# Two rows of token scales sent through DRAM on GpSimd's queue instead of through TensorE, in a two-block transformer kernel

## The chip, the cores and the metric

One NeuronCore of a Trainium2 chip runs the whole kernel. The metric is the time of one execution on the device in microseconds (us). The kernel before takes 914.07 us, the median of 3 runs (914.02 to 915.09).

## What is computed

The input is 256 tokens of width 1024 (float32), beside two memories of 256 tokens. Two blocks run one after the other: each is a mixer, a cross-attention on a memory and a feed-forward, every one behind an RMS norm and added to the running state. The two places that matter here are the input projections of the second block's mixer and of its feed-forward, which is the last layer of the kernel:

```python
x = x + hybrid_mixer(rms_norm(x, norm_mix_g), w_in, ...)      # q, k, v, z, ... = split(h @ w_in)
x = x + memory_cross_attention_2(rms_norm(x, norm_xa_g), ...)
x = x + swiglu(rms_norm(x, norm_ffn_g), w_gate, w_up, w_down) # (silu(h @ w_gate) * (h @ w_up)) @ w_down
return rms_norm(x, final_g)
```

`rms_norm` multiplies each token by one number, 1 / sqrt(mean(x^2) + eps). The kernel doesn't apply it ahead of a projection. It multiplies the raw state by the gain, projects, and puts the token's scale on the result, so that the scale can be worked out while TensorE is at the projection.

## The kernel before, in words

**Weights.** All matrices come as 146 slabs of 1 MB through a ring of four buffers (`w_ring`, `load`, L405, on SyncE's queue). ScalarE rounds a slab to `w_hi` (`hi`, L1227), VectorE takes the rest into `w_lo` (`lo`, L1719), and TensorE makes each product in three passes from the two halves of both operands. A slab is loaded into the place of slab i - 4 when TensorE has used that one (`slab_used`).

**Layouts.** A projection comes out either with tokens on the partitions, where a token's scale is a number per partition (`r_mix2`, `r_ff2`: 128 partitions x 2 blocks of tokens), or with features on the partitions and tokens along the free axis (`form_a`, L609 to L611, and `form_a_pair`, L646 and L650). There the scales are needed as a row of 256 numbers repeated on all 128 partitions: `r_row[:, 0, :]`.

**How the row is made.** `scales_on_diagonal(r)` on VectorE (L1756) writes for each block of tokens a 128 x 128 matrix with the scales on the diagonal. `spread` on TensorE (L744 to L751) multiplies a matrix of ones with it, so that every partition of a PSUM bank holds the row. `row_copy` on ScalarE (L1260 to L1262) copies it to `r_row`. It is done for four rows: ROW_MIX and ROW_CONV (first block, which the change leaves alone), ROW_MIX2 (second mixer) and ROW_FF2 (last feed-forward).

**Order around ROW_MIX2** (slabs I_SBQK to I_SBQK + 3 are q and k, I_SBV the two slabs of v). Every engine's order is written out by hand. TensorE: I_SBQK, + 1, + 2, then `spread`, then I_SBQK + 3, for which it waits until VectorE has summed the halves of I_SBQK + 1 (`sum_halves`, L2122), then the two slabs of I_SBV, then I_ZU. VectorE: `r_mix2` (last step L2115), the diagonal, `lo(I_SBQK + 3)`, `sum_halves(1)`, `lo(I_SBQK + 4)`, `sum_halves(2)`, the wait for the row (L2137), `scaled_qk(0)` to `(2)` (L2131), and then `lo(I_SBQK + 5)`, which TensorE needs for the second slab of I_SBV. ScalarE: `row_copy` stands between `half_of(I_SBQK + 2)` and `hi(I_SBQK + 6)`.

**Order around ROW_FF2.** TensorE: gate and up of the first group of 256 hidden columns (I_FF2, I_FF2 + 1), `spread`, gate and up of the second group (`glu_in(ff2_gate(1))`), then `glu_out`, the down-projection of the first group (slab I_FF2 + 4, L609 to L611), for which it waits for `glu_lo` and for that slab's `w_lo`. VectorE: `r_ff2`, then inside `boundary` one more slab (`lo(nxt + 3)`), the diagonal, two `half_add` (L2328), the wait for the row (L2340), and `glu(0)`: gate times row (L2341), gate times up (L2353), `ff_l` (L2358), `lo(nxt + 2)`, which is slab I_FF2 + 4. ScalarE in `glu(0)`: Silu (L1659), `ff_h` (L1668), `hi(nxt + 2)`.

**GpSimd** has done its constants and the rotary angles by then. Its queue holds a few DMAs that repeat a row of DRAM on all partitions: two final gains (L521, `load_gain`), `ln_g`, `ln_b`, `b_sp` (L590 to L592), and at the start one that brings the 256 positions to 128 x 2, one number at a time (L535, `pos_i`). Its last instruction is the load of the last gain, which waits for VectorE's `gain_used` (L2107).

Of the kernel before, what the change touches and what calls it, by code (L numbers as in the profile page):

```python
# [28 lines left out]
F32 = mybir.dt.float32  # L29
# [6 lines left out]
P = 128  # L36
D = 1024
S = 256
# [65 lines left out]
ROW_MIX, ROW_CONV, ROW_MIX2, ROW_FF2 = range(4)  # L104
# [65 lines left out]
def build(nc, a, out):  # L170

    with ExitStack() as ctx:
# [7 lines left out]
        def new(name, shape, dt=F32):  # L180
            t = at(name, shape, cursor[0], dt)
            cursor[0] += -(-int(np.prod(shape[1:])) // 8) * 8
            return t
# [22 lines left out]
        r_row = new("r_row", [P, 2, S])  # L206
# [88 lines left out]
        def stats(n):  # L295
            used[0] += n
            assert used[0] <= 256
            return stat[:, used[0] - n:used[0]]
# [5 lines left out]
        r_mix, r_mem, r_mem2, r_xa, r_mlp, r_f, r_mix2, r_ff2 = (stats(2) for _ in range(8))  # L304
# [6 lines left out]
        def tok(b):  # L311
            return ps[:, b, :]
# [25 lines left out]
        def sem(name):  # L338
            return ctx.enter_context(nc.semaphore(name))
# [13 lines left out]
        diag_ready, row_t, row_ready = sem("diag_ready"), sem("row_t"), sem("row_ready")  # L353
# [33 lines left out]
        gate_ready, merge_done, merged_hi, merged_lo = sem("gate_ready"), sem("merge_done"), sem("merged_hi"), sem("merged_lo")  # L387
        last_sq, sum_ready, root_ready, y_ready, out_lead, out_tail, stored = (sem(x) for x in ("last_sq", "sum_ready", "root_ready", "y_ready", "out_lead", "out_tail", "stored"))
        u_scaled = sem("u_scaled")
        gain_product, last_gain = sem("gain_product"), sem("last_gain")  # L390

        block = ctx.enter_context(nc.Block())
# [122 lines left out]
        def _(pool):  # L515
            def load_gain(n):
                if n > 0:
                    pool.wait_ge(gain_used, n)
                w = a[GAIN_ROWS[n]]
                w = w if len(w.shape) == 1 else w.squeeze(0)  # L520
                pool.dma_start(gain[:, :], w.partition_broadcast(P)).then_inc(gain_loaded, 16)  # L521
# [49 lines left out]
            for part in (TWO_PI_A, TWO_PI_B, TWO_PI_C):  # L571
# [17 lines left out]
            load_gain(G_F)  # L589
            pool.dma_start(ln_g[:, :], a["sgu_ln_g_2"].squeeze(0).partition_broadcast(P)).then_inc(sgu_loaded, 16)  # L590
            pool.dma_start(ln_b[:, :], a["sgu_ln_b_2"].squeeze(0).partition_broadcast(P)).then_inc(sgu_loaded, 16)
            pool.dma_start(b_sp[:, :, :], a["b_spatial_2"].squeeze(0).rearrange("g t -> (g t)").partition_broadcast(P)  # L592
                           .rearrange("p (g t) -> p g t", g=SGU_GROUPS)).then_inc(sgu_loaded, 16)

# [4 lines left out]
            pool.wait_ge(xo_ready, XA_HEADS)  # L599
            pool.memset(y3_pad[:, :, 0:CONV3 - 1], 0.0).then_inc(pad3_ready, 1)  # L600
            load_gain(G_FINAL)


        @block.tensor
        def _(pe):
# [32 lines left out]
            def form_a_pair(i, bank, step=0, ready=(), low_ready=None):  # L638

                pe.wait_ge(hi_done, weight_count(i) + step)  # L640
                wh, wl = slab(i, 256)
                for k in range(KD):
                    if ready:
                        ready(k)
                    for b in range(2):
                        pe.matmul(feat(bank + b), wh[:, k, b * P:(b + 1) * P], xx[:, k, :, :].rearrange("p e t -> p (e t)"), start=k == 0, stop=False)  # L646
                pe.wait_ge(lo_done, weight_count(i) + step)
                for b in range(2):
                    for k in range(KD):
                        mm = pe.matmul(feat(bank + b)[:, 0:S], wl[:, k, b * P:(b + 1) * P], xx[:, k, 0, :], start=False, stop=k == KD - 1)  # L650
                mm.then_inc(slab_used, 1)
# [88 lines left out]
            def raw_ready(n):  # L740

                return [lambda k, done=done: pe.wait_ge(done, 16 * (n - R_XA) + 9 + k) for done in (raw_hi, raw_lo)]

            def spread(m, bank):  # L744

                pe.wait_ge(ones_set, 1)
                pe.wait_ge(const_ready, 1)
                for tb in range(TB):
                    pe.wait_ge(diag_ready, 2 * m + tb + 1)
                    mm = pe.matmul(bank[:, tb * P:(tb + 1) * P], ones[:, :], diag[:, tb, :], start=True, stop=True)  # L750
                mm.then_inc(row_t, 1)  # L751
# [287 lines left out]
            form_a(I_SBQK, (0,), x_t, 256, 0, *raw_ready(R_MIX2))  # L1039
            form_a_pair(I_SBQK + 1, 2)  # L1040
            form_a_pair(I_SBQK + 2, -4)
            spread(ROW_MIX2, tok(3))
            pe.wait_ge(pair_sum, FF_PAIRS + 1)
            form_a_pair(I_SBQK + 3, 2)
            pe.wait_ge(pair_sum, FF_PAIRS + 2)
# [53 lines left out]
            form_a_pair(I_ZU, 0)  # L1099
            pe.wait_ge(pair_sum, FF_PAIRS + 3)  # L1100
            form_a_pair(I_ZU + 1, 2)
            pe.wait_ge(row_ready, 2)
            form_b_half(I_ZV, 2, x_t)
            beside(I_ZV + 1)
            for j in range(4):
# [26 lines left out]
            for n, br in enumerate(BRANCH_ORDER):  # L1132
                for half in range(2):
                    i = I_BR + 6 * n + 3 * half
                    r = 2 * n + half
# [15 lines left out]
                    for kk in range(4):  # L1151
                        for tb in range(TB):
                            t = slice(tb * P, (tb + 1) * P)
# [19 lines left out]
            def glu_in(i, gate_done=None, up_done=None, step=0, ready=(), last=False):  # L1173
                if gate_done is not None:
                    pe.wait_ge(glu_sum, 2 * gate_done - 1)
                form_a_pair(i, 0, step, *ready[1:])
                if up_done is not None:
                    pe.wait_ge(glu_sum, 2 * up_done)
                if last:
                    form_a(i + 1, (2,), x_t, step=step)  # L1180
                else:
                    form_a_pair(i + 1, 2, step)
# [4 lines left out]

            pe.wait_ge(xo_lo, 8)
            glu_in(I_FF2, ready=raw_ready(R_FF2))
            spread(ROW_FF2, tok(0))  # L1190
            glu_in(ff2_gate(1), gate_done=1, up_done=1)
            pe.wait_ge(row_ready, 3)
            glu_out(ff2_gate(1) + 2, 1, first=True)
            with pe.Fori(0, 2) as t:
                for c in range(2, 6):
# [18 lines left out]
        def _(act):  # L1214
# [45 lines left out]
            def row_copy(m, bank):  # L1260
                act.wait_ge(row_t, m + 1)
                act.activation(r_row[:, 0, :], bank[:, 0:S], ACT.Copy).then_inc(row_ready, 1)  # L1262
# [145 lines left out]
            for tb in range(TB):  # L1408
                t = slice(tb * P, (tb + 1) * P)
# [152 lines left out]
            half_of(I_SBQK + 1, 6, qk_half[1])  # L1562
            hi(I_SBQK + 5)
            half_of(I_SBQK + 2, 0, qk_half[2])
            row_copy(ROW_MIX2, tok(3))
            hi(I_SBQK + 6)
            half_of(I_SBQK + 3, 6, qk_half[3])
            hi(I_SBQK + 7)
# [35 lines left out]
            for n in range(BRANCHES):  # L1604
                for half in range(2):
                    i = I_BR + 6 * n + 3 * half
                    r = 2 * n + half
# [36 lines left out]

            half_copy(0, I_FF2)
            half_copy(1, I_FF2 + 1)
            row_copy(ROW_FF2, tok(0))

            def glu(g, i, first=False, last=False, step=0, turn=0):

# [55 lines left out]
        def _(dve):  # L1706
# [47 lines left out]
            def scales_on_diagonal(r):  # L1754
                for tb in range(TB):
                    dve.tensor_scalar(diag[:, tb, :], ident[:, :], r[:, tb:tb + 1], None, ALU.mult).then_inc(diag_ready, 1)  # L1756
# [130 lines left out]
            t = [rope_t[:, j, :, :].rearrange("p t (g f) -> p t g f", f=ROPE_HALF) for j in range(4)]  # L1887
# [95 lines left out]
            for tb in range(TB):  # L1983
                t = slice(tb * P, (tb + 1) * P)
# [9 lines left out]
            for tb in range(TB):  # L1994
                t = slice(tb * P, (tb + 1) * P)
                dve.tensor_tensor(c_acc[:, :, t], c_acc[:, :, t], feat(2)[:, t].unsqueeze(1).broadcast_to([P, 4, P]), ALU.mult).then_inc(conv_normed, 1)
            lo(29)
            for tb in range(TB):
                t = slice(tb * P, (tb + 1) * P)
# [113 lines left out]
            after(dve.tensor_scalar(nv, nv, 1.0 / D, EPS, ALU.mult, ALU.add))  # L2113
            rsqrt(nv, r_mix2, nt)
            after(dve.tensor_tensor(r_mix2, r_mix2, r_f, ALU.mult))  # L2115
            scales_on_diagonal(r_mix2)
            lo(I_SBQK + 3)

            def sum_halves(n, bank, dst):
# [14 lines left out]
            sum_halves(1, 6, qkT2[:, 2:4, :])  # L2134
            lo(I_SBQK + 4)
            sum_halves(2, 0, qkT2[:, 4:6, :])
            dve.wait_ge(row_ready, 2)  # L2137
            for j in range(3):
                scaled_qk(j)
            lo(I_SBQK + 5)  # L2140
# [59 lines left out]
            for tb in range(TB):  # L2200
                dve.wait_ge(vg_ready, tb + 1)
                six, two = bn6[:, 6 * tb:6 * tb + 6], bn2[:, 2 * tb:2 * tb + 2]
                v, y, t = nv[:, tb:tb + 1], ny[:, tb:tb + 1], nt[:, tb:tb + 1]
# [81 lines left out]
            for n in range(BRANCHES):  # L2285
                for half in range(2):
                    i = I_BR + 6 * n + 3 * half
                    r = 2 * n + half
# [14 lines left out]
                    m = merged[:, :, half * HALF:(half + 1) * HALF]  # L2303
# [16 lines left out]
            after(dve.tensor_scalar(r_xa, r_xa, XA_SCALE, None, ALU.mult))  # L2320
            x_attention(1, I_O2)
            boundary(R_FF2, UPD[I_O2], I_O2 + 3, Q_FF2, r_ff2, I_FF2)
            scales_on_diagonal(r_ff2)

            def half_add(c, n):

# [7 lines left out]
            def glu(g, i, first=False, last=False, step=0):  # L2334

                nxt = ff2_gate(1) if first else i + 3
                if not first:
                    half_add(0, 2 * g + 1)
                if first:
                    dve.wait_ge(row_ready, 3)  # L2340
                dve.tensor_tensor(blocks(ff_u[:, 1, :]), blocks(ff_s[:, 0, :]), row_of_scales(0), ALU.mult).then_inc(glu_in_ready, 1)  # L2341
                if last:
                    lo(N_SLABS - 1)
                elif not first:
                    lo(nxt, step)
                if last:
                    dve.wait_ge(slab_used, i + 2 + step)
                elif not first:
                    half_add(1, 2 * g + 2)
                dve.wait_ge(silu_ready, g + 1)  # L2350
                if not first:
                    dve.wait_ge(glu_lo, g)
                dve.tensor_tensor(ff_u[:, 0, :], feat(2) if last else ff_s[:, 1, :], ff_r[:, 0, :], ALU.mult).then_inc(glu_ready, 1)  # L2353
                if not first and not last:
                    lo(nxt + 1, step)
                dve.wait_ge(glu_hi, g + 1)
                f = slice(2, 4) if last else slice(0, 2)
                dve.tensor_tensor(ff_l[:, f, :], blocks(ff_u[:, 0, :]), ff_h[:, f, :].bitcast(F32), ALU.subtract).then_inc(glu_lo, 1)  # L2358
                if not last:
                    lo(nxt + 2, step)  # L2360
# [85 lines left out]
```

## Time and profile before

| | |
|---|---|
| median of 3 runs | 914.07 us |
| span of the profiled execution, first to last instruction | 910.9 us |
| the profiled execution's own time | not recorded; 3.2 us lie between its span and the median |
| TensorE busy with matmuls | 901.4 us, 99% of the span |
| VectorE, ScalarE, GpSimd busy | 661.6, 504.2, 24.3 us |
| DMA | 164.38 MB, mean 180 GB/s |
| granted TensorE clock | 0.999 of full speed |

Lines of the profile give a start and a duration on one engine. PE is TensorE's matmuls, PEld its weight loads, DVE VectorE, ACT ScalarE, POOL GpSimd, SPq SyncE's DMA queue. L with a number is the line of the kernel; helpers such as `lo` give one line for all their uses. Matmuls are pipelined, so one that starts every 0.23 us is shown 0.39 us long.

### The profile page before, as it was taken

How to read it: one execution, taken by the hardware profiler on the slowest of the kernel's cores; microseconds unless marked ns; L12 is line 12 of the kernel's file. 1: busy time of each engine (PE TensorE's matmuls, PEld its weight loads, DVE VectorE, ACT ScalarE, POOL GpSimd, SP SyncE). 2: the span in 40 equal slices, each digit the busy share in tenths (PEclk: the TensorE clock that was granted, in tenths of full speed). 3: DMA queues.
4: the chain of work that ended last, by engine and by line, in shares of the span. 5: the costliest groups of instructions: out<-in, count | busy, mean ns of one | idle time of the engine just before them, and what ended most of it. 6: DMA issues, size and time to landing. Idle time of an engine off the chain costs nothing.

```text
span 910.9 us, 12836 instructions
## 1 busy us (share of the span) xinstructions
PE 901.4 (99%) x5160; PEld 787.4 (86%) x5160; DVE 661.6 (73%) x920; ACT 504.2 (55%) x584; POOL 24.3 (3%) x69
## 2 busy tenths in 40 slices
PE   9999999999999999999999999999999999999997
PEld 8888998889888888888888988888899888888886
DVE  5799999987577666656967996646686676565665
ACT  6796435655555444445656757744464654544444
POOL 1600010000000000000000000000000000000000
PEclk9999999999999999999999999999999999999999
DMA  9746555454355666654755455455453456666551
GB/s 353 253 159 223 183 199 185 139 185 140 92 186 186 195 199 197 190 185 153 238 188 183 159 166 183 152 175 187 173 185 103 144 183 191 196 193 197 189 185 47
DMA packets 101280, 164.38 MB, mean 180 GB/s; under 512 B 2736, under 2 KB 71088, under 8 KB 101104
## 3 DMA queue, kind: packets, MB, share of 16 engines
q1 hardware_dynamic: 100528, 161.71, 54.2%
q0 software_dynamic: 560, 1.84, 0.7%
q8 instruction: 34, 0.56, 0.3%
q10 hardware_dynamic: 144, 0.16, 0.1%
q14 instruction: 14, 0.11, 0.0%
HBM read 162.65 MB, written 1.05 MB: 180 GB/s over the span
## 4 chain that ended last, share of the span: by engine, by line
PE 92%; DVE 5%; DMA 2%; ACT 1%; issue 1%; SPq 0%; DVEq 0%; ACTq 0%
PE ps L609 20%; PE ps L611 19%; PE ps L610 19%; PE ps L646 18%; PE ps L650 9%; DVE w_lo L1719 1%; DVE c_acc L1865 1%; DMA w_ring<-in_w_in 1%; PE ps L737 1%; DMA head_raw<-in_head 1%; PE ps L857 0%; ACT w_hi L1227 0%; PE ps L774 0%; DVE mem_l L1734 0%; PE ps L826 0%
## 5 line engine op out<-in xcount | busy, mean ns | idle before, releaser
L1719 DVE TENSOR_TENSOR w_lo<-w_ring,w_hi 128x2048 fp32r<-128x2048 f32 x146 | 333.4, 2288 | 114.2 <-ACT w_hi L1227 113.2
L1227 ACT ACTIVATE w_hi<-w_ring 128x2048 fp32r<-128x2048 f32 x146 | 278.6, 1911 | 88.3 <-DMA w_ring<-in_w_in 27.3
L646 PE MATMUL ps<-xx,w_hi 128*128 128x512 f32 x720 | 171.8, 391 | 0.3
L646 PEld LDWEIGHTS ps<-xx,w_hi 128*128 128x128 f32 x720 | 133.3, 188 | 27.4 <-issue 0.7
L609 PE MATMUL ps<-w_hi,xx 128*128 128x512 f32 x304 | 120.2, 395 | 0.0
L611 PE MATMUL ps<-w_hi,xx 128*128 128x512 f32 x304 | 118.6, 390 | 0.0
L610 PE MATMUL ps<-w_lo,xx 128*128 128x512 f32 x304 | 118.5, 390 | 0.0
L650 PEld LDWEIGHTS ps<-xx,w_lo 128*128 128x128 f32 x720 | 92.3, 191 | 3.5
L650 PE MATMUL ps<-xx,w_lo 128*128 128x256 f32 x720 | 93.4, 283 | 0.0
L609 PE MATMUL ps<-w_hi,ff_h 128*128 128x512 f32 (+1 forms) x218 | 84.7, 389 | 0.0
L610 PE MATMUL ps<-w_lo,ff_h 128*128 128x512 f32 (+1 forms) x218 | 84.6, 388 | 0.0
L611 PE MATMUL ps<-w_hi,ff_l 128*128 128x512 f32 (+1 forms) x218 | 84.4, 387 | 0.0
L611 PEld LDWEIGHTS ps<-w_hi,xx 128*128 128x128 f32 x304 | 57.1, 188 | 12.1
L609 PEld LDWEIGHTS ps<-w_hi,xx 128*128 128x128 f32 x304 | 57.1, 188 | 11.7 <-issue 0.5
L610 PEld LDWEIGHTS ps<-w_lo,xx 128*128 128x128 f32 x304 | 57.2, 188 | 11.1
L609 PE MATMUL ps<-xx,w_hi 128*128 128x256 f32 x200 | 56.9, 285 | 0.0
L610 PE MATMUL ps<-xx,w_hi 128*128 128x256 f32 x200 | 56.6, 283 | 0.0
L611 PE MATMUL ps<-xx,w_lo 128*128 128x256 f32 x200 | 56.6, 283 | 0.0
L1865 DVE SCALAR_TENSOR_TENSOR c_acc<-u_pad,cols,c_acc 128x256 f32<-128x256 f32 x120 | 49.3, 476 | 0.2 <-DVE stat L1727 0.2
L611 PEld LDWEIGHTS ps<-w_hi,ff_l 128*128 128x128 f32 x218 | 40.9, 188 | 8.5
L609 PEld LDWEIGHTS ps<-w_hi,ff_h 128*128 128x128 f32 x218 | 41.0, 188 | 8.1 <-DVE ff_l L2080 0.2
L610 PEld LDWEIGHTS ps<-w_lo,ff_h 128*128 128x128 f32 x218 | 41.0, 188 | 7.6
(339 smaller groups left out, 1335.9 us busy)
## 6 DMA issues: line engine op xcount, KB each, us to landing
w_ring<-in_w_in SPq DMA_DIRECT2D x34, 1024.0 KB, 5.1
w_ring<-in_mlp_up_w SPq DMA_DIRECT2D x16, 1024.0 KB, 5.6
w_ring<-in_mlp_down_w SPq DMA_DIRECT2D x16, 1024.0 KB, 4.9
w_ring<-in_w_gate_ffn SPq DMA_DIRECT2D x11, 1024.0 KB, 5.3
w_ring<-in_w_up_ffn SPq DMA_DIRECT2D x11, 1024.0 KB, 5.3
w_ring<-in_w_down_ffn SPq DMA_DIRECT2D x11, 1024.0 KB, 4.9
w_ring<-in_xkv_w SPq DMA_DIRECT2D x8, 1024.0 KB, 5.4
w_ring<-in_w_out SPq DMA_DIRECT2D x8, 1024.0 KB, 4.8
```

What stands on the lines that cost most here:

```text
L609: pe.matmul(o, lh, rh, start=first, stop=False)
L610: pe.matmul(o, lh, rl, start=False, stop=False)
L611: return pe.matmul(o, ll, rh, start=False, stop=last)
L646: pe.matmul(feat(bank + b), wh[:, k, b * P:(b + 1) * P], xx[:, k, :, :].rearrange("p e t -> p (e t)"), start=k == 0, stop=False)
L650: mm = pe.matmul(feat(bank + b)[:, 0:S], wl[:, k, b * P:(b + 1) * P], xx[:, k, 0, :], start=False, stop=k == KD - 1)
L737: mm = pe.transpose(ps[:, bank, (k - k0) * P:(k - k0 + 1) * P], h[:, tb, k * P:(k + 1) * P], ident[:, :])
L1227: act.activation(w_hi[:, s, :], w_ring[:, s, :], ACT.Copy).then_inc(hi_done, 1)
L1719: dve.tensor_tensor(w_lo[:, s, :], w_ring[:, s, :], w_hi[:, s, :].bitcast(F32), ALU.subtract).then_inc(lo_done, 1)
L1865: ins = dve.scalar_tensor_tensor(c_acc[:, c, :], win, tap, c_acc[:, c, :], ALU.mult, ALU.add)
```

## The change

For ROW_MIX2 and ROW_FF2 the diagonals, `spread` and `row_copy` are taken out. VectorE raises a semaphore where the diagonals stood. GpSimd, at the end of its program, waits for it, writes the 256 scales to a row of a DRAM tensor, waits until that has landed, and reads the row back into `r_row[:, 0, :]` on all 128 partitions. VectorE waits for that second DMA where it waited for `row_copy`.

```diff
+        scales_ready, row_moved = sem("scales_ready"), sem("row_moved")
...
+            def scales_row(m, r):
+
+                row = a["scales"][m - ROW_MIX2]
+                pool.wait_ge(scales_ready, m - 1)
+                pool.dma_start(row.rearrange("(t p) -> p t", p=P), r, allow_slow_non_contiguous=True).then_inc(row_moved, 16)
+                pool.wait_ge(row_moved, 32 * (m - ROW_MIX2) + 16)
+                pool.dma_start(r_row[:, 0, :], row.partition_broadcast(P)).then_inc(row_moved, 16)
...
             load_gain(G_FINAL)
+            scales_row(ROW_MIX2, r_mix2)
+            scales_row(ROW_FF2, r_ff2)
...
             form_a_pair(I_SBQK + 2, -4)
-            spread(ROW_MIX2, tok(3))
...
             form_a_pair(I_ZU + 1, 2)
-            pe.wait_ge(row_ready, 2)
...
             glu_in(I_FF2, ready=raw_ready(R_FF2))
-            spread(ROW_FF2, tok(0))
             glu_in(ff2_gate(1), gate_done=1, up_done=1)
-            pe.wait_ge(row_ready, 3)
...
             half_of(I_SBQK + 2, 0, qk_half[2])
-            row_copy(ROW_MIX2, tok(3))
...
             half_copy(1, I_FF2 + 1)
-            row_copy(ROW_FF2, tok(0))
...
             after(dve.tensor_tensor(r_mix2, r_mix2, r_f, ALU.mult))
-            scales_on_diagonal(r_mix2)
+            dve.sem_inc(scales_ready, 1)
...
-            dve.wait_ge(row_ready, 2)
+            dve.wait_ge(row_moved, 32)
...
             boundary(R_FF2, UPD[I_O2], I_O2 + 3, Q_FF2, r_ff2, I_FF2)
-            scales_on_diagonal(r_ff2)
+            dve.sem_inc(scales_ready, 1)
...
-                    dve.wait_ge(row_ready, 3)
+                    dve.wait_ge(row_moved, 64)
...
+    aps["scales"] = nc.dram_tensor("scales", (2, S), F32, kind="Internal").ap()
```

## Rows read from the trace of the kernel before

**Rows 1.** The page: the span, and TensorE's busy time with its share of it

```profile
span 910.9 us, 12836 instructions
PE 901.4 (99%) x5160; PEld 787.4 (86%) x5160; DVE 661.6 (73%) x920; ACT 504.2 (55%) x584; POOL 24.3 (3%) x69
```

**Rows 2.** Who waited for whom, TensorE's matmuls: us in total, times, longest

```profile
PE ps L821 <- POOL ones L524: 1.1, 1, 1.1
...
PE ps L609 <- DVE w_lo L1719: 0.5, 1, 0.5
```

**Rows 3.** Chain that ended last, at the two spreads: start us, us, what

```profile
451.25 0.45 PE ps L750 x4
...
732.84 0.44 PE ps L750 x4
```

**Rows 4.** By tile, diagonals and row copies: ns min/median/max, first and last start

```profile
L1756 DVE TENSOR_SCALAR diag<-ident,stat x8: 278/282/290, 24.8 to 732.0; 128x128 f32<-128x128 f32 x8
...
L1262 ACT ACTIVATE r_row<-ps x3: 377/379/386, 30.1 to 733.4; 128x256 f32<-128x256 f32 x3
```

**Rows 5.** Timeline at the second mixer: start us, us, engine, line, operation [idle before]

```profile
447.59 0.16 DVE L2115 TENSOR_TENSOR stat<-stat 128x2 f32<-128x2 f32 x1
...
450.39 0.68 DVE L2122 TENSOR_TENSOR qkT<-ps,qkT 128x512 f32<-128x512 f32 x1
...
454.07 0.68 DVE L2131 SCALAR_TENSOR_TENSOR qkT<-ps,r_row 128x512 f32<-128x512 f32 x1
...
455.87 2.29 DVE L1719 TENSOR_TENSOR w_lo<-w_ring,w_hi 128x2048 fp32r<-128x2048 f32 x1
...
462.57 0.39 PE L609 MATMUL ps<-w_hi,xx 128*128 128x512 f32 x1
```

**Rows 6.** Timeline at the last feed-forward, same columns

```profile
729.60 2.29 DVE L1719 TENSOR_TENSOR w_lo<-w_ring,w_hi 128x2048 fp32r<-128x2048 f32 x1
...
732.56 0.53 PEld L750 LDWEIGHTS ps<-diag,ones 128*128 128x128 f32 x4
...
734.30 0.69 DVE L2341 TENSOR_TENSOR ff_u<-ff_s,r_row 128x512 f32<-128x512 f32 x1
...
736.99 1.90 ACT L1227 ACTIVATE w_hi<-w_ring 128x2048 fp32r<-128x2048 f32 x1
...
738.92 2.29 DVE L1719 TENSOR_TENSOR w_lo<-w_ring,w_hi 128x2048 fp32r<-128x2048 f32 x1 [1.11 <-ACT w_hi L1227]
...
744.15 0.19 PEld L609 LDWEIGHTS ps<-w_hi,ff_h 128*128 128x128 f32 x1
```

**Rows 7.** DMA issues: queue, times, KB each, us from issue to landing

```profile
gain<-in_norm_f_w POOLq DMA_DIRECT2D x1, 512.0 KB, 4.1
gain<-in_final_g POOLq DMA_DIRECT2D x1, 512.0 KB, 5.7
...
out<-xn ACTq DMA_DIRECT2D x1, 160.0 KB, 2.3
pos_i<-in_positions POOLq DMA_DIRECT2D x1, 1.0 KB, 5.4
```

**Rows 8.** Timeline: VectorE ends its work, GpSimd issues the last gain

```profile
438.15 2.36 DVE L2105 TENSOR_TENSOR xn<-h,gain 128x1024 f32<-128x1024 f32 x2
...
440.86 0.53 POOL L521 DMA_DIRECT2D gain<-in_final_g  x1 [198.47 <-DVEq L2107]
```

**Rows 9.** DMA queues from 440 to 444.3 us: packets, MB, share of 16 engines

```profile
q1 hardware_dynamic: 461, 0.94, 70.7%
```

**Rows 10.** Stretches of the last feed-forward: us, busy by engine, PEclk, DMA share, GB/s

```profile
732.00:734.00 2.00, 2.00 (x15) 1.87 (x15) 1.30 (x4) 1.11 (x3) 0.00 (x0) 1.00 0.00 0
734.00:737.70 3.70, 3.70 (x21) 3.17 (x21) 2.23 (x4) 2.93 (x4) 0.00 (x0) 1.00 0.93 279
737.70:739.40 1.70, 1.70 (x14) 1.57 (x13) 0.59 (x2) 1.69 (x2) 0.00 (x0) 1.00 0.03 10
739.40:743.40 4.00, 4.00 (x23) 3.48 (x22) 3.10 (x3) 0.92 (x3) 0.00 (x0) 1.00 0.87 262
```

## The prediction

> **What bounds the kernel now.** I read the page first: TensorE is busy in 901.4 of 910.9 us [rows 1]. The list of waits says that what is left isn't waiting on others: the longest wait of a matmul is 1.1 us at the start, and the only other wait I show is 0.5 us for a `w_lo` [rows 2]. So the kernel is one unbroken queue of matmuls. Work taken from TensorE shortens it by its own length, work taken from VectorE or ScalarE by nothing, and a wait that reaches TensorE lengthens it in full. The reader is to keep two questions apart: what the spreads cost TensorE, and whether a row that comes later reaches TensorE as a wait. The chain of waits answers the first, the timelines and the DMA views the second.
>
> **Removed from TensorE.** The chain that ended last passes through both spreads, for 0.45 and 0.44 us [rows 3]. TensorE must be free to use them. At the mixer it goes on only when the sum at L2122 is ready, which ends at 451.07 [rows 5], just after the spread begins; the two diagonals ahead of it on VectorE, 2 x 0.28 us one behind the other, about 0.4 us on the timeline since their ends overlap [rows 4], go too, so the sum comes at about 450.7. At the feed-forward the sum that TensorE needs moves by the same 0.4 us. I take 0.45 at each place: **-0.9 us** if no row is late. The diagonals and the row copies (0.38 us each on ScalarE, [rows 4]) are worth nothing by themselves; TensorE's 99% covers them. The waits for `row_ready` on TensorE had long been met and cost nothing.
>
> **Added.** Each row now takes: VectorE's semaphore to GpSimd, a scattered store of 1 KB, a semaphore, a read of 128 KB onto 128 partitions, a semaphore. VectorE to GpSimd took 0.35 us for the last gain (440.51 to 440.86, [rows 8]). The two other hops I estimate at 0.1 us. That last gain stands ahead in GpSimd's program; it landed 5.7 us after 440.86 [rows 7], at 446.6, before the first scales are ready, and nothing stands behind the new DMAs. GpSimd's waiting therefore delays only the rows.
>
> The store and the read are not in the trace. From above the nearest rows are `pos_i`, the same 256 single numbers the other way, at 5.4 us, and a gain at 5.7; from below the shortest DMA of all, 2.3 us [rows 7]. The first gain, 512 KB in 4.1 us, bears on both: a slab of 1 MB moves in some 3.7 us (279 GB/s, [rows 10]), half a slab in 1.9, so some 2.2 us are fixed. That gives 2.2 + 0.5 = 2.7 for 128 KB and, with `pos_i`'s issue being slower, about 2.5 for the store, where the DMA engines are free. They often aren't. The last gain was issued at 440.86, yet until 444.3 the DMA engines moved packets of queue 1, the slab loads, alone [rows 9]. I read this as a rule of this kernel: a DMA of GpSimd waits for the slab that is under way. Here the Trainium skill says otherwise ("DMA: Bandwidth & Descriptors", Queues, rings and completion order): each DMA engine takes turns between its queues after every packet, by which the small DMAs would hardly wait; that is a rival below.
>
> **The mixer's row.** The scales are there at 447.75, GpSimd issues at 448.1. With the middles between free and caught (2.5 to 5.4: 4.0; 2.7 to 5.7: 4.2) and two hops the row lands at 456.5, where it was wanted at 454.07 [rows 5]. Behind VectorE's wait stand three scalings and `lo(I_SBQK + 5)`: before, 454.07 to 458.16, so 4.1 us. It would now end at 460.7. TensorE wants that slab at 462.57 [rows 5], now 462.1. Cover: 1.4 us. With both ends high (5.4 + 5.7) the row lands at 459.4 and TensorE waits 1.5 us. I take no wait: **-0.45 us**.
>
> **The feed-forward's row.** VectorE's semaphore comes behind `lo(nxt + 3)`, which ends at 731.89 [rows 6], 2.3 us after the scales are known. GpSimd issues at 732.24. The DMA engines are idle from 732 to 734 [rows 10]; the store's packets pass ahead of the next slab, and it lands at 734.75. The read is issued at 734.85, in the middle of that slab, which holds the engines until 737.7 [rows 10]; 0.5 us of its own data and some 0.2 to land: 738.4, and VectorE goes on at 738.5, not at 734.30. From there the chain can be read off: L2341 starts at 734.30, Silu, the product and `ff_h` follow, ScalarE's `w_hi` runs 736.99 to 738.89, VectorE's `w_lo` of the slab for `glu_out` ends at 741.21 [rows 6]. That is 6.9 us from the row to a ready slab; before, it ended 2.9 us ahead of TensorE's need at 744.15. Now it ends at 745.4, so `glu_out` starts about 745.45, 1.3 us later than before: the saved 0.45 is gone too, and TensorE stands for 1.75 us. **+1.3 us**. With 2.3 for both DMAs it starts at 744.0 (-0.15), with 5.4 and 5.7 at 750.5 (+6.35). Later groups don't add to this: behind `glu_out` come 5.5 us of matmuls, before the next sum is wanted, and VectorE is idle for a third of these stretches [rows 10].
>
> **Sum**: -0.45 + 1.3 = +0.85 us. The span of the profiled execution, 910.9, becomes 911.8; the median stands 3.2 us above that span, and with the same distance it becomes 914.9. With all bounds low -0.6, with all high +7.85.
>
> **Rivals.**
>
> 1. *The row is hardly late.* The read takes turns with the slab: 734.85 + 2.7 = 737.55, chain to 744.55, +0.45 at the feed-forward, 0.0 in sum: 914.1. With both DMAs at 2.3: 913.5. The overtaking is against rows 9. By the skill's rule of turns and the same page's (Anatomy of one DMA) 2.0 us fixed plus bytes at 436 GB/s, an estimate from the page alone gives a row at 736.8 and 913.2.
>
> 2. *Slower: the store is caught as well.* Place: GpSimd's queue at 734. It decides from the point where the store's packets are ready later than 734.0, that is over 1.75 us after the issue. Then the store follows the slab and lands at 738.2, the read is issued at 738.3 and lands at 741.0 if it is ahead of the next slab: chain to 748.0, +3.9, sum +3.4, 917.5. If the read is caught as well (the next slab moves from about 739.4 to 743.4, [rows 10]) it lands at 744.2, `glu_out` starts at 751.3, +7.1, sum +6.7, 920.8. `pos_i`, caught in the loads of the start, with 5.4 us, speaks for it; the idle stretch 732 to 734 against it. TensorE would then stand for 4.3 to 7.5 us; the granted clock is 1.00 in all stretches here [rows 10], and whether it falls after such a gap the trace doesn't show.
>
> 3. *The mixer's row is late too*: up to +1.5 us there in place of 0, so +2.8 in sum, 916.9. Both DMAs must take over 9.7 us together.
>
> 4. *The change does nothing where it says*: TensorE can't use the freed 0.45 us because another wait (the sum at L2122, or a slab) ends last there. Then +0.9 on the sum, 915.8.
>
> **Chances.** The likeliest case 0.45 (its own range 913.9 to 915.8), rival 1 0.17, rival 2 0.29, rival 3 0.05, rival 4 0.04. About 0.2% of the time, 1.8 us, is what a measurement of this kernel can tell from no change. The likeliest case with rivals 1 and 4 stays within it but for the late end of the first: 0.57. Slower by more: rivals 2 and 3 and that end, 0.40. Faster by more than 1.8 us needs twice what both spreads cost: 0.03. Predicted is the likeliest case, 914.9. The range goes from 913.3, both rows in time, to 920.8, both DMAs of the feed-forward caught.
>
> **What the profile after would show.** L750 gone in both places and TensorE going on 0.45 us earlier behind I_SBQK + 2. Two issues of about 0.9 and 0.5 us on POOL at 448 and 732, each pair over 5 to 8 us apart from issue to last landing. L2131 starting at about 456 without a gap on TensorE at 462. L2341 near 738, VectorE idle for some 4 us ahead of it, and a gap of 1.5 to 2 us ahead of L609 where it stood at 744.15, put down to VectorE's `w_lo`. I am wrong if that gap is absent (rows in time) or longer than 3 us, if the row's landing doesn't follow the end of a slab, or if there is a gap at the mixer.

## The result and the profile after

The changed kernel takes 931.39 us (median of 4 runs, 930.16 to 931.57) against 914.05 for before: a ratio of 1.019, 95% interval 1.0178 to 1.0202. I had forecast 914.9 with a range to 920.8. The mechanism of the forecast is there (the row is late, and TensorE stands ahead of `glu_out`), but at both places and several times as long.

The page of the changed kernel, to be read against [rows 1]:

```profile
span 929.8 us, 12817 instructions
...
PE 905.3 (97%) x5152; PEld 789.9 (85%) x5152; DVE 660.9 (71%) x916; ACT 503.3 (54%) x582; POOL 27.1 (3%) x73
...
PEclk9999999999999999999989999999999979999999
```

The span grew by 18.9 us, the median by 17.3. The difference lies in the kernel before: the execution of it that was profiled was a quick one. In the later rounds its executions with a span of 910.9 us took 912.9 to 913.1 us, 2.0 to 2.2 above the span, and not the 3.2 that I had added. TensorE's busy time grew too, although work was taken from it; the clock row says why: in two slices the granted clock is below 0.9. Who waited for whom, in us in total, times and longest:

```profile
POOL r_row L599 <- DMA scales<-stat: 17.1, 2, 9.0
PE ps L620 <- DVE w_lo L1724: 15.3, 3, 8.5
DVE ff_u L2346 <- DMA r_row<-scales: 11.2, 1, 11.2
...
DVE qkT L2136 <- DMA r_row<-scales: 10.1, 1, 10.1
```

Together they are the path of the loss: GpSimd waits for its store, VectorE for the read, and TensorE for a `w_lo` that stands behind VectorE's wait. In [rows 2] the same matmul line (L609 there, L620 here) waited 0.5 us. The DMA issues, KB each and median us from issue to landing:

```profile
r_row<-scales POOLq DMA_DIRECT2D x2, 128.0 KB, 6.5
...
scales<-stat POOLq DMA_DIRECT2D x2, 1.0 KB, 9.0
```

The timeline at the mixer, beside [rows 5]:

```profile
448.42 0.74 POOL L597 DMA_DIRECT2D scales<-stat  x1 [6.71 <-DVEq L2121]
...
458.13 0.57 POOL L599 DMA_DIRECT2D r_row<-scales  x1 [8.97 <-DMA scales<-stat]
...
462.67 1.91 ACT L1234 ACTIVATE w_hi<-w_ring 128x2048 fp32r<-128x2048 f32 x1 [8.85 <-DMA w_ring<-in_w_in]
...
464.62 0.69 DVE L2136 SCALAR_TENSOR_TENSOR qkT<-ps,r_row 128x512 f32<-128x512 f32 x1 [10.08 <-DMA r_row<-scales]
...
466.43 2.29 DVE L1724 TENSOR_TENSOR w_lo<-w_ring,w_hi 128x2048 fp32r<-128x2048 f32 x1
...
468.77 0.79 PE L620 MATMUL ps<-w_hi,xx 128*128 128x512 f32 x1 [6.13 <-DVE w_lo L1724]
```

The scaling starts at 464.62 and not at 454.07; the second slab of v starts at 468.77 and not at 462.57. A line that I had not looked for is ScalarE's: it waited 8.85 us for a slab, so the slab loads are late as well. The timeline at the last feed-forward, beside [rows 6]:

```profile
737.62 2.29 DVE L1724 TENSOR_TENSOR w_lo<-w_ring,w_hi 128x2048 fp32r<-128x2048 f32 x1
737.95 0.72 POOL L597 DMA_DIRECT2D scales<-stat  x1 [279.26 <-DVEq L2328]
...
746.80 0.56 POOL L599 DMA_DIRECT2D r_row<-scales  x1 [8.13 <-DMA scales<-stat]
...
753.50 0.69 DVE L2346 TENSOR_TENSOR ff_u<-ff_s,r_row 128x512 f32<-128x512 f32 x1 [11.24 <-DMA r_row<-scales]
...
758.08 2.29 DVE L1724 TENSOR_TENSOR w_lo<-w_ring,w_hi 128x2048 fp32r<-128x2048 f32 x1 [1.11 <-ACT w_hi L1234]
...
760.52 0.76 PE L620 MATMUL ps<-w_hi,ff_h 128*128 128x512 f32 x1 [8.53 <-DVE w_lo L1724]
```

And the stretches of TensorE's two gaps with what follows each (us, busy by engine, PEclk, DMA share, GB/s):

```profile
462.60:468.70 6.10, 0.04 (x1) 0.00 (x0) 4.08 (x5) 4.30 (x3) 0.00 (x0) 0.75 0.89 308
468.70:472.60 3.90, 3.83 (x9) 3.05 (x10) 3.87 (x5) 0.00 (x0) 0.00 (x0) 0.52 0.00 0
751.90:760.40 8.50, 0.09 (x1) 0.00 (x0) 4.40 (x5) 3.54 (x4) 0.00 (x0) 0.73 0.58 203
760.40:766.00 5.60, 5.48 (x13) 4.35 (x14) 3.07 (x3) 4.27 (x4) 0.00 (x0) 0.50 0.01 3
```

The granted clock falls inside each gap and stays at about 0.5 (1.2 GHz) behind it. There matmuls start every 0.43 us, not every 0.23: 9 of them take 3.87 us in place of 2.04, 13 take 5.60 in place of 2.95, so 1.8 and 2.7 us are lost. The account of the span: gaps 6.1 + 8.5, slow clock 1.8 + 2.7, less the 0.7 that the two spreads turned out to be worth (below), is 18.4 of 18.9 us; another 0.3 us lies ahead of the change, since the last gain is issued at 441.17 where it was 440.86 [rows 8], and 0.2 us I can't place.

### The profile page after: what moved, and what is told of

Same layout as the page of the kernel before. It is cut to its first block, busy times and chain, and to the rows that moved or that the text cites. A ratio compares the mean times of both kernels' runs of the same rounds, so it can differ in the third digit from the quotient of the medians.

```text
span 929.8 us, 12817 instructions
## 1 busy us (share of the span) xinstructions
PE 905.3 (97%) x5152; PEld 789.9 (85%) x5152; DVE 660.9 (71%) x916; ACT 503.3 (54%) x582; POOL 27.1 (3%) x73
## 4 chain that ended last, share of the span: by engine, by line
PE 85%; DVE 7%; DMA 4%; issue 2%; ACT 2%; SPq 0%; POOL 0%; DVEq 0%; POOLq 0%; ACTq 0%
PE ps L620 19%; PE ps L621 19%; PE ps L622 19%; PE ps L657 15%; PE ps L661 8%; DVE w_lo L1724 3%; DMA r_row<-scales 1%; DVE c_acc L1870 1%; DMA scales<-stat 1%; DMA w_ring<-in_w_in 1%; PE ps L748 1%; ACT w_hi L1234 1%; DMA head_raw<-in_head 1%; PE ps L837 1%; DVE xx L1750 0%
## 5 line engine op out<-in xcount | busy, mean ns | idle before, releaser
L620 PE MATMUL ps<-w_hi,xx 128*128 128x512 f32 x304 | 121.1, 398 | 6.1 <-DVE w_lo L1724 6.1
L620 PE MATMUL ps<-w_hi,ff_h 128*128 128x512 f32 (+1 forms) x218 | 85.9, 394 | 8.5 <-DVE w_lo L1724 8.5
L620 PEld LDWEIGHTS ps<-w_hi,xx 128*128 128x128 f32 x304 | 57.6, 189 | 18.5 <-DVE w_lo L1724 6.5
L620 PE MATMUL ps<-xx,w_hi 128*128 128x256 f32 x200 | 56.9, 285 | 0.0
L620 PEld LDWEIGHTS ps<-w_hi,ff_h 128*128 128x128 f32 x218 | 41.7, 191 | 17.0 <-issue 8.7
```

The lines of the kernel that those rows point to most:

```text
L620: pe.matmul(o, lh, rh, start=first, stop=False)
```

## The experiments

Two questions: why does the store take 9 us, and does what it does to the slabs cost anything by itself? Theory A: the store's form, 256 writes of 4 B side by side, is slow. Theory B: it only waits behind the slab under way. Theory C: any store of GpSimd's queue to DRAM is slow.

**1. One place alone.** In the first kernel only the mixer's row goes through DRAM, in the second only the feed-forward's; the other is made as before.

```diff
             scales_row(ROW_MIX2, r_mix2)
-            scales_row(ROW_FF2, r_ff2)
...
```

> Only the mixer's row goes through DRAM; the feed-forward's row is made by diagonal, spread and copy as before. The trace of the changed kernel shows 6.2 us of standing and 1.8 us of slow matmuls at the mixer. If the two places are independent: +8.0 us on the span, about 922 us in all. If the loss at the mixer only shows together with the other (a shared queue or semaphore): near 914 us.

> Only the feed-forward's row goes through DRAM. By the trace of the changed kernel +8.3 us of standing and 2.5 us of slow matmuls: +10.9 us, about 925 us, and with the mixer's +8.0 the whole +18.9. If the mixer's delay also pushed this place (late slabs carried on): less than +9.

Measured: 921.21 us (ratio 1.0077, 1.006 to 1.0094) and 923.87 (1.0115, 1.0097 to 1.0133), before beside them 913.42. The losses, 7.8 and 10.5 us, add to 18.2 (7.79 + 10.45), where both together cost 17.3 against a median of before that stood 0.6 us higher in that round; TensorE's gaps are 5.9 and 8.3 us, those of the changed kernel 6.1 and 8.5. Within what the runs can tell the two places are independent, and each is to be explained alone.

**2. The store alone, with nobody behind it.** The kernel before, its rows still made by TensorE; GpSimd stores the scales at the same moments.

```diff
...
+                pool.wait_ge(scales_ready, m + 1)
+                pool.dma_start(row.rearrange("(t p) -> p t", p=P), r, allow_slow_non_contiguous=True).then_inc(row_moved, 16)
+                pool.wait_ge(row_moved, 16 * m + 16)
...
```

> The kernel before with both rows still made by TensorE; GpSimd also stores the 256 scales to DRAM at both places, one number at a time, and nobody but GpSimd waits. Theory A (the store is itself slow and holds up the slab loads beside it): the store lands after 8 to 10 us, the slab under way then takes about 10 us instead of 5.1, and the time stays within 1 us of before, since the slabs have that much slack. Theory B (the store only waits behind the slab under way): it lands in at most 5.4 us, slabs land as before, time as before. If late slabs alone stall TensorE: several us slower.

Measured: 913.67 us, ratio 1.0005 (0.9996 to 1.0015), and the stores landed after 9.0 us in the median. The stretch 452 to 459 us (same columns as above) in the kernel before, in the changed one, and in this one:

```profile
452.00:459.00 7.00, 7.00 (x40) 6.10 (x39) 6.20 (x7) 4.10 (x5) 0.00 (x0) 1.00 0.51 164
```

```profile
452.00:459.00 7.00, 7.00 (x40) 6.11 (x39) 2.01 (x2) 1.82 (x2) 0.57 (x1) 1.00 0.28 38
```

```profile
452.00:459.00 7.00, 7.00 (x41) 6.09 (x40) 6.54 (x6) 2.40 (x3) 0.00 (x0) 1.00 0.25 36
```

The last two numbers of each line are the share of the DMA engines and the GB/s. For 7 us a store of 1 KB lets the slab loads do 38 and 36 GB/s in place of 164. Theory B's 5.4 us are refuted. The time is unchanged, so at these two places the late slabs as such cost nothing; they have slack. What costs is VectorE's wait.

**3. Prices on quiet engines.** The kernel before; when all output is stored, GpSimd issues eight DMAs one by one. They lengthen the kernel, so its own time says nothing here.

```diff
+            pool.wait_ge(stored, 16 * 3)
+            pool.dma_start(sc[0].rearrange("(t p) -> p t", p=P), r, **scattered).then_inc(row_moved, 16)
+            moved()
...
```

> The kernel before; when all output is stored and no other DMA runs, GpSimd issues eight DMAs one after the other, each waited for: store of 256 x 4 B to DRAM (as in the change), 128 x 8 B, 128 x 4 B, 256 x 4 B each 512 B apart, one piece of 512 B from one partition, 256 x 4 B from DRAM to partitions, 128 x 8 B within SBUF, 1 KB of DRAM onto 128 partitions. Theory A (the cost is the many small writes to DRAM): the first takes 7 us or more even here, 128 pieces about half of that beyond a fixed part, the single piece 2 to 3 us, the DMAs into SBUF 2 to 3 us. Theory B (waiting behind slabs): all eight take 2.3 to 3 us. Theory C (any store to DRAM on this queue is slow to be confirmed): all five stores alike, 7 us or more.

The timeline of GpSimd in this kernel (start, then the time for issuing; each DMA is issued when the one before has landed, so the distance of two starts is a price with its semaphore):

```profile
911.44 0.73 POOL L613 DMA_DIRECT2D scales<-stat  x1 [469.45 <-DMA out<-xn]
920.07 0.57 POOL L615 DMA_DIRECT2D scales<-stat  x1 [7.89 <-DMA scales<-stat]
923.57 0.54 POOL L617 DMA_DIRECT2D part<-stat  x1 [2.93 <-DMA scales<-stat]
931.36 0.71 POOL L619 DMA_DIRECT2D apart<-stat  x1 [7.26 <-DMA part<-stat]
933.59 0.51 POOL L621 DMA_DIRECT2D whole<-ones  x1 [1.52 <-DMA apart<-stat]
935.44 0.74 POOL L623 DMA_DIRECT2D pv<-scales  x1 [1.33 <-DMA whole<-ones]
938.17 0.54 POOL L625 DMA_DIRECT2D pt<-stat  x1 [1.99 <-DMA pv<-scales]
940.09 0.54 POOL L627 DMA_DIRECT2D r_row<-scales  x1 [1.38 <-DMA pt<-stat]
```

The change's store costs 8.6 us with nothing else running, so theory B doesn't explain it. Theory C doesn't either: the same 256 numbers put 512 B apart cost 2.2 us, 128 pairs of 8 B 3.5, 128 numbers of 4 B 7.8, one piece of 512 B 1.9, 256 numbers from DRAM to partitions (the form of `pos_i`) 2.7. It isn't the count either, since half as many numbers cost nearly the same. My "about half of that" for 128 pieces was wrong for the 4 B ones. The read that ends the row took 3.5 us to land.

**4. How far apart.** The same store with 4, 8, 16, 32, 64 and 128 B from one number to the next, and the 4 B form on ScalarE's queue.

```diff
+            pool.dma_start(a["pitch1"][:, 0:1].rearrange("(t p) w -> p (t w)", p=P), r_f, allow_slow_non_contiguous=True).then_inc(row_moved, 16)
+            moved()
+            pool.dma_start(a["pitch2"][:, 0:1].rearrange("(t p) w -> p (t w)", p=P), r_f, allow_slow_non_contiguous=True).then_inc(row_moved, 16)
+            moved()
...
```

> The kernel before; after all output is stored GpSimd stores the same 256 x 4 B to DRAM six times, each waited for, with 4, 8, 16, 32, 64 and 128 B from one number to the next; then ScalarE's queue does the 4 B form; then 128 pieces of 8 B with 64 B between; then 1 KB of DRAM (an input) onto 128 partitions. If writes into the same stretch of DRAM wait for one another and that stretch is 64 B: about 8.3 us at 4 B, 3 to 5 at 8 and 16 B, 2 us from 64 B on. If the stretch is longer (256 or 512 B): still above 3 us at 64 B. If the 4 B spacing alone is the slow form: 2 us from 8 B on. If GpSimd's software queue has a part in it, ScalarE's store is much shorter than 8.3 us; if it is the DRAM's doing, 7 to 8.5 us as well.

The timeline of GpSimd, then two of the DMA issues:

```profile
911.65 0.73 POOL L612 DMA_DIRECT2D pitch<-stat  x1 [469.50 <-DMA out<-xn]
919.78 0.73 POOL L614 DMA_DIRECT2D pitch<-stat  x1 [7.39 <-DMA pitch<-stat]
923.76 0.71 POOL L616 DMA_DIRECT2D pitch<-stat  x1 [3.25 <-DMA pitch<-stat]
925.99 0.72 POOL L618 DMA_DIRECT2D pitch<-stat  x1 [1.52 <-DMA pitch<-stat]
```

```profile
hard<-stat ACTq DMA_DIRECT2D x1, 1.0 KB, 7.4
pairs<-stat POOLq DMA_DIRECT2D x1, 1.0 KB, 1.7
```

8.1 us at 4 B, 4.0 at 8 B, 2.2 at 16 B (2.2, 2.2 and 2.0 at 32, 64 and 128 B). ScalarE's hardware queue needs 7.4 us for the 4 B form, so GpSimd's software queue has no part in it. Pairs that start 64 B apart land in 1.7 us, side by side they took 3.5. All twelve stores of single numbers or pairs in these two kernels fit one rule, by the distance from the start of one write to the next: at 4 B 7.4 to 8.6 us, at 8 B 3.5 to 4.0, at 16 B or more 1.7 to 2.2 (the 7.4 and the 1.7 are times to landing). None of the three outcomes that I had written down for the spacing came: by the one with a stretch of 64 B the 16 B form should have taken 3 to 5 us. One can count the same as 16, 8 and at most 4 writes to 64 B, but no run tells such a stretch from the plain distance. That the writes wait for one another in the memory is my reading of this; the runs show the times and the slowed loads beside them, not the place. The Trainium skill ("DMA: Bandwidth & Descriptors", Specifications) says that transfers under 512 B are done as read-modify-write. Such a rule fits slow small writes, but by itself it would make the spaced ones slow as well, and they took 2.2 us.

**5. The store's spacing in the changed kernel.** All waits and all work are kept; the store goes 512 B apart, and the read fetches another input, so the rows don't hold the tokens' scales.

```diff
-                row = a["scales"][m - ROW_MIX2]
+                row = a["norm_f_w"][0:S]
...
-                pool.dma_start(row.rearrange("(t p) -> p t", p=P), r, allow_slow_non_contiguous=True).then_inc(row_moved, 16)
+                pool.dma_start(a["apart"][:, 0:1].rearrange("(t p) w -> p (t w)", p=P), r, allow_slow_non_contiguous=True).then_inc(row_moved, 16)
```

> The changed kernel, but the store puts its 256 numbers 512 B apart in a DRAM tensor that nobody reads, and the read takes 1 KB of another input instead (so the second mixer's q and k, its gates and the last feed-forward are scaled with numbers that aren't the tokens' scales; all work and all waits are kept). If the cost is many 4-byte writes into the same few hundred bytes: the store lands after 2 to 4 us, the slab beside it in about 5.3 us, no gap at the mixer or under 1 us, at the feed-forward a gap of 2 to 5 us: 915 to 919 us. If a GpSimd store to DRAM is slow beside slab loads whatever its addresses: 8 to 9 us again and about 931 us.

Measured: 914.10 us, ratio 1.0001 (0.9991 to 1.001). Its DMA issues and the only gap on TensorE at the two places:

```profile
r_row<-in_norm_f_w POOLq DMA_DIRECT2D x2, 128.0 KB, 5.3
apart<-stat POOLq DMA_DIRECT2D x2, 1.0 KB, 2.8
...
745.71 0.47 PE L620 MATMUL ps<-w_hi,ff_h 128*128 128x512 f32 x1 [1.17 <-DVE w_lo L1724]
```

The waits, the work and the sizes are those of the changed kernel, so the 17 us hang on where 256 numbers are put in DRAM. The read's source was changed too; experiment 9 reads the stored row itself, its read takes 5.6 us, and the time stays within 2 us of this one. The time is below the 915 to 919 us that theory A gave here, by 1 us, and the gap at the feed-forward, 1.2 us, below its 2 to 5.

**6. Pairs, and an earlier semaphore.** Stored as they lie (8 B pairs, side by side) and turned by a VectorE copy; in the second kernel the feed-forward's semaphore also stands ahead of the last `lo` of `boundary`.

```diff
-                pool.dma_start(row.rearrange("(t p) -> p t", p=P), r, allow_slow_non_contiguous=True).then_inc(row_moved, 16)
+                pool.dma_start(row.rearrange("(p t) -> p t", t=TB), r).then_inc(row_moved, 16)
...
+                if n == R_FF2:
+                    dve.sem_inc(scales_ready, 1)
                 if n not in (R_XA, R_MLP):
                     lo(nxt + 3)
```

> The changed kernel with the scales stored as they lie, 128 pieces of 8 B, read back in that order and turned into token order by one VectorE copy (0.3 to 0.5 us). On quiet engines this store took 3.2 us and the change's 8.3. If the store's form is the cause: it lands in 3 to 5 us here, the slab beside it isn't held up by more than 1 us, time 916 to 921. If not: about 931.

> As e6_pairs, and VectorE raises the feed-forward's semaphore as soon as the scales are known, ahead of the slab's w_lo (2.3 us). If the feed-forward's gap is the row's lateness one for one, TensorE stands 2.3 us less than in e6_pairs: 914 to 919. If the two DMAs are tied to the slabs' rhythm (a read leaves when a slab is through), the gain is 0 or a whole wait for a slab.

Measured: 921.11 us (1.008, 1.0063 to 1.0097) and 921.58 (1.009, 1.0072 to 1.0107). The middle form costs the middle: stores 5.4 us in the median, over the 3 to 5 that I gave, reads 5.0, gaps on TensorE of 1.6 and 3.5 us. At the mixer it was 7.2 us from the store's issue to the read's, and ScalarE had the slab beside it at 459.37, where before it had it at 456.33: 2.6 us late once the 0.5 us by which this trace lags is taken off, against my "not more than 1 us". The earlier semaphore brought nothing, and the timeline of the first of the two, where the semaphore stands behind the `w_lo`, says why (the changed kernel's own, 737.62 and 737.95 above, says it too):

```profile
731.58 2.29 DVE L1724 TENSOR_TENSOR w_lo<-w_ring,w_hi 128x2048 fp32r<-128x2048 f32 x1
...
731.90 0.54 POOL L597 DMA_DIRECT2D scales<-stat  x1 [275.59 <-DVEq L2333]
```

GpSimd issues 0.3 us after the `w_lo` *starts*. The semaphore instruction behind it doesn't wait for its end.

**7. The same prices beside slab loads**, in the first feed-forward.

```diff
+            pool.wait_ge(raw_lo, 32)
+            pool.dma_start(sc[0].rearrange("(t p) -> p t", p=P), r, **scattered).then_inc(row_moved, 16)
+            moved()
...
```

> The kernel before, with the eight DMAs of e4_prices_quiet in the same order in the first feed-forward, beside the slab loads. If waiting behind a slab is a cost of its own: each takes 0 to 3.5 us more than its quiet price (8.3, 3.2, 7.5, 1.9, 1.6, 2.4, 1.6, 3.5 us). The slabs beside the first and third take 8 us or more, the others about 5.3. TensorE may stand a few us where a slab comes late.

```profile
258.24 0.74 POOL L612 DMA_DIRECT2D scales<-stat  x1 [14.97 <-DVE xx L1772]
268.24 0.57 POOL L614 DMA_DIRECT2D scales<-stat  x1 [9.27 <-DMA scales<-stat]
278.31 0.54 POOL L616 DMA_DIRECT2D part<-stat  x1 [9.50 <-DMA scales<-stat]
287.52 0.71 POOL L618 DMA_DIRECT2D apart<-stat  x1 [8.68 <-DMA part<-stat]
292.55 0.51 POOL L620 DMA_DIRECT2D whole<-ones  x1 [4.32 <-DMA apart<-stat]
```

The slow form costs 10.0 us (8.6 quiet), the spaced one 5.0 (2.2), the single piece 4.6 (1.9), and the read landed after 5.2 (3.5). So standing beside slabs adds 1.4 to 2.9 us to six of the eight, and nothing to the form of `pos_i` (2.7 both times). Theory B's wait exists beside theory A. One was outside what I gave: the pairs, 10.1 us against 3.5. From their issue at 268.24 until 274 us queue 1 moved 760 packets of the slabs that the first store had held back, and GpSimd's queue 2 of its 32; most of the others moved from 274 to 276. So the pairs seem to have paid for the store ahead of them; no run has them there without it.

The one run took 918.03 us, and here late slabs did reach TensorE. A slab issued at 273.30, beside these stores, took 9.0 us to land. The chain of waits goes from it over `w_hi`, `w_lo` and the scales' steps to a gap of 2.4 us at 289.7. The slack that covered one such store at each of two places in experiment 2 didn't cover three in a row.

**8. The most that this route could give.** The spaced store with the earlier semaphore.

```diff
+                if n == R_FF2:
+                    dve.sem_inc(scales_ready, 1)
...
-            dve.sem_inc(scales_ready, 1)
```

> As e5_apart (numbers stored 512 B apart, 1 KB of another input read in their place, so the rows aren't the tokens' scales), and VectorE raises the feed-forward's semaphore ahead of the slab's w_lo. This is the best that a route through DRAM in two DMAs could be. If both rows now come in time: TensorE keeps the 0.9 us of both spreads, 913.2 against 914.1 for before. If the read still waits for a slab: as e5_apart, 914 to 915.

Measured: 914.21 us, ratio 1.0002 (0.9992 to 1.0011). The chain of waits of this kernel has the read and, behind it, the 6.9 us of VectorE and ScalarE:

```profile
732.00 5.57 DMA r_row<-in_norm_f_w
...
744.69 0.47 PE ps L620
```

The read was issued with the DMA engines free and still took 5.6 us. Its first packets moved after 733.0, a slab issued at 732.50 joined in after 734.0, from then on both queues moved packets side by side, and the slab took 7.8 us. Even a quick store doesn't win back the spreads.

**9. A route that gives the right numbers without the slow form.** Pairs that start 16 B apart; the row is read with its gaps (2 KB) and VectorE picks the numbers out. Near its start GpSimd fills the DRAM tensor once, so that the gaps hold numbers. First for both rows (with the earlier semaphore), then for the mixer's alone.

```diff
...
-                pool.dma_start(row.rearrange("(t p) -> p t", p=P), r, allow_slow_non_contiguous=True).then_inc(row_moved, 16)
+                pool.dma_start(row[:, 0:TB], r).then_inc(row_moved, 16)
...
-                pool.dma_start(r_row[:, 0, :], row.partition_broadcast(P)).then_inc(row_moved, 16)
+                pool.dma_start(row_in[:, :], row.rearrange("q w -> (q w)").partition_broadcast(P)).then_inc(row_moved, 16)
...
+                after(dve.tensor_copy(r_row[:, 0, :].rearrange("p (t q) -> p t q", t=TB), row_in[:, :].rearrange("p (q w) -> p w q", w=2 * TB)[:, 0:TB, :]))
...
```

> A route through DRAM with the right numbers and without the slow form: the scales are stored as 128 pairs of 8 B, 16 B apart (four writes to 64 B), the row with its gaps (2 KB) is read onto 128 partitions, and VectorE picks the numbers out (0.3 to 0.5 us). The feed-forward's semaphore is raised ahead of the slab's w_lo. If at most four writes to 64 B is what makes a store quick: it lands in 1.7 to 4 us, the read in 3.5 to 6, time 914 to 917. If pairs are held up beside slab loads for another reason: as e7_pairs_early, 921.

> The same route for the mixer's row alone, the feed-forward's row by diagonal, spread and copy as before. The mixer's row may land up to about 458.0 us before TensorE waits: if it does, the 0.45 us of one spread stay, 913.6 against 914.0, under what 5 rounds can tell apart. If the read is caught by the slab of 458 to 462 us: 915 to 918.

Measured: 915.84 us (ratio 1.0023, 1.0008 to 1.0039) and 913.39 us (1.0003, 0.9991 to 1.0014). DMA issues of the first, and its gap at the feed-forward:

```profile
row_in<-scales POOLq DMA_DIRECT2D x2, 256.0 KB, 5.6
...
scales<-stat POOLq DMA_DIRECT2D x2, 1.0 KB, 2.9
...
746.27 0.47 PE L625 MATMUL ps<-w_hi,ff_h 128*128 128x512 f32 x1 [1.30 <-DVE w_lo L1729]
```

The same route, with a tensor of twice the size in DRAM, is 15.5 us quicker than the change. For the mixer's row alone it can't be told from before. No version that I ran beats before by more than the runs can tell.

## Why the prediction was wrong, by its own steps

**"What bounds the kernel" held.** TensorE is one unbroken queue; a wait that reached it cost its full length, and late slabs that didn't reach it cost nothing (913.67).

**"Removed from TensorE", -0.45 us at each place, held, and was a little less.** At both places TensorE's last group of the slab ahead of the spread and its next slab start 1.91 us apart (449.54 and 451.45, 733.20 and 735.11), where they were 2.28 us apart before (449.17 and 451.45, 730.76 and 733.04): 0.37 us each.

**"Added": this is the step that failed.** It took the store at 2.5 us (4.0 at the mixer) between bounds of 2.3 and 5.4. It landed after 9.4 us at the mixer and 8.6 at the feed-forward. I took `pos_i` for the upper bound because it has the same 256 numbers. But it goes the other way, and on quiet engines that way costs 2.7 us where the store costs 8.6. The rows from before that I used held no store of small pieces to DRAM side by side, so none of them bounded this price from above; I should have let the upper end stand open, or said that it was a guess. What the runs showed in its place is a cost by spacing: 8.1, 4.0 and 2.2 us at 4, 8 and 16 B.

**The read**, 2.7 to 5.7, was too low as well: 6.5 us at both places, 3.5 and 3.2 on quiet engines. Here the store acts a second time: its slowed slabs are still going when the read is issued. That is worth about 1 us, since behind a spaced store the reads still took 5.1 to 5.8. From 459 to 462.4 us, just after the read's issue at 458.13, the DMA engines of the changed kernel moved queue 1 alone:

```profile
q1 hardware_dynamic: 1047, 1.06, 94.7%
```

That a GpSimd DMA stands behind the slab under way was read rightly from [rows 9], and experiment 7 puts 1.4 to 2.9 us on it. The Trainium skill's rule of turns between queues ("DMA: Bandwidth & Descriptors", Queues, rings and completion order) isn't borne out in that stretch. In experiment 8, where the read's packets came ahead of the slab's, both queues did move packets in the same microsecond (from 734 to 735 us 16 and 67), as that rule has it.

**The semaphore at the feed-forward** I placed at the end of `lo(nxt + 3)`, 2.3 us after the scales. It comes 0.3 us after that `w_lo` starts. This error went the other way: with it right and all else as forecast, the store would have been issued at about 729.9. In experiment 5, where the store is quick, this error of 2.3 us and the read's (5.5 us where 3.55 was forecast) nearly cancel. That its time, 914.10, lies so near to the 914.9 of the forecast, and its gap of 1.2 us to the 1.75, is luck in part.

**The chains behind the row held.** At the mixer, 464.62 to 468.72, the 4.1 us that I gave; at the feed-forward, 753.50 to 760.37, 6.9 us. The wants of TensorE (462.1, 743.7) held too. With the measured DMAs put into the sum, 448.1 + 9.7 + 6.5 gives a row at 464.3 at the mixer and a gap of 6.3 us; it was 6.1.

**The clock** I named in rival 2 and left without a price. It cost 1.8 and 2.7 us, a quarter of the loss. The Trainium skill ("TensorE: Matmul & The Clock Gate", Why this matters for your kernels) warns of idle gaps between bursts of matmuls for this reason. The trace agrees, with a granted clock of 0.50 to 0.52 behind gaps of 6.1 and 8.5 us, and 1.00 throughout with the gaps of 1.2 and 1.3 us in the kernels with spaced stores. Experiment 6 lies between: 1.00 behind its gap of 1.6 us, but 0.62 in the 2.6 us behind that of 3.5.

**The rivals.** Rival 3 (the mixer's row late too) had the right place with TensorE standing for at most 1.5 us; it stood for 6.1, and with the clock the place cost 7.8. Rival 2 had the right sign but the wrong hinge: what decided wasn't whether the store's packets came ahead of the slab's at 734.0. On quiet engines, with no slab to catch it, the store takes 8.6 us as well. I gave the two 0.34 together, and the range ended at 920.8 because all prices in it ended at rows of other operations. I had also named a gap at the mixer, and one of over 3 us at the feed-forward, as signs of being wrong; both came.

## What to carry to other kernels

Before a small tile is scattered to DRAM, look at how far apart the writes start. At 4 and 8 B a store of 1 KB cost 8 and 4 us here, and the 4 B form slowed the loads beside it; at 16 B and more it cost 2. Spacing the numbers out was enough, as long as the reader can skip the gaps. And a price has a bound only from an operation of the same direction and form; where the trace has none, measure it alone at the end of the kernel, where nothing else runs.

## What the runs showed of the hardware that I had not expected

- Beside a 1 KB store of single 4 B numbers the slab loads moved 36 to 38 GB/s for 7 us, where they moved 164 before.
- On ScalarE's hardware queue that store takes as long: 7.4 us.
- A semaphore instruction of VectorE behind a 2.29 us operation reached GpSimd 0.3 us after that operation began.
- Reading 1 KB of DRAM onto 128 partitions takes 3.2 to 3.5 us on quiet engines, and 4.1 to 6.6 beside slabs.
